# First stage of a two-block network: input products of high and low parts, own keys ahead of the context's

## The reference, cut to what matters

```python
proj = hm @ w_in                                   # 1024 x 1792: q 512, k and v 256, u 512, gate 512
q = rms_norm(proj[..., :512].reshape(b, n, 8, 64), q_g)
k, v = split_kv(proj[..., 512:768], k_g)
q, k = apply_rope(q, ...), apply_rope(k, ...)
k, v = concatenate([context's k, v], [k, v])       # context_kv(hcn, w_in, k_g): the same 256 columns
attn = block_attention(q, k, v)
g = u * sigmoid(gate)
g = silu(layer_norm(depthwise_conv(g, conv_w) + conv_b, ln_g, ln_b))     # 31 taps
out = concatenate([attn, g], -1) @ w_out
```

## Time and profile before

| | us |
|---|---|
| median of 3 runs (lowest, highest) | 1674.82 (1673.35, 1675.28) |
| the profiled execution | 1671.44 |
| its span in the trace | 1669.6 |
| PE, DVE, ACT, POOL busy in the span | 1471.2, 481.2, 339.5, 110.6 |
| first product of the changed part starts | 36.76 |
| first scores of the loop start | 105.62 |
| first use of an expert chunk | 233.29 |

### The profile page before, as it was taken

How to read it: one execution, slowest core, us unless ns; L and a number is a source line. 1 busy time by engine, 2 the same in 40 slices (tenths; PEclk the granted TensorE clock), 3 DMA queues, 4 the chain that set the end, 5 groups by cost and what they waited for, 6 DMA issues and landing times. The chain is left out here.

```text
span 1669.6 us, 17591 instructions
## 1 busy us (share of the span) xinstructions
PE 1471.2 (88%) x7708; PEld 824.5 (49%) x7708; DVE 481.2 (29%) x732; ACT 339.5 (20%) x515; POOL 110.6 (7%) x109
## 2 busy tenths in 40 slices
PE   4999979889888899789798878978888999999999
PEld 2755642232232343289532323323324767788897
DVE  1496540100100000156500001001004754345443
ACT  1122410000000000143200000000003645544442
POOL 0000000000000000010000000000003044330000
PEclk9999989999989999999799999999999999999999
DMA  9989959999999999996399999999999844244510
GB/s 374 410 359 413 410 216 429 414 429 427 416 428 427 412 428 429 407 398 234 126 418 422 427 430 419 429 427 423 428 424 355 291 175 149 104 148 168 189 51 26
DMA packets 93298, 563.06 MB, mean 337 GB/s; under 512 B 8048, under 2 KB 9448, under 8 KB 53670
## 3 DMA queue, kind: packets, MB, share of 16 engines
q1 hardware_dynamic: 89504, 551.77, 81.2%
q0 software_dynamic: 2384, 9.42, 1.6%
q10 hardware_dynamic: 1334, 0.75, 0.2%
HBM read 558.74 MB, written 3.17 MB: 337 GB/s over the span
## 5 line engine op out<-in xcount | busy, mean ns | idle before, releaser
L2207 PE MATMUL ps<-ring,scratch 128*32 128x512 f32 x2048 | 434.6, 610 | 54.4 <-DMA ring<-in_moe_w_up 26.1
L2207 PEld LDWEIGHTS ps<-ring,scratch 128*32 128x32 f32 x2048 | 129.2, 112 | 346.7 <-issue 339.5
L2186 PE MATMUL ps<-ring,scratch 128*32 128x512 f32 x1024 | 205.8, 603 | 29.7 <-DMA ring<-in_moe_w_down 29.7
L1927 PE MATMUL ps<-ring_parts,scratch_parts 128*128 128x512 f32 x656 | 186.6, 402 | 5.0 <-DVE xT_parts L1189 1.4
L1927 PE MATMUL ps<-scratch_parts,ring_parts 128*128 128x256 f32 x704 | 146.0, 282 | 0.0
L1927 PEld LDWEIGHTS ps<-ring_parts,scratch_parts 128*128 128x128 f32 x656 | 122.4, 189 | 33.1 <-DVE xT_parts L1189 1.6
L2186 PEld LDWEIGHTS ps<-ring,scratch 128*32 128x32 f32 x1024 | 50.3, 111 | 160.8 <-issue 107.8
L607 ACT ACTIVATE ring_parts<-ring 128x2048 fp32r<-128x2048 f32 x56 | 106.4, 1919 | 93.1 <-PE ps L1927 86.6
L460 DVE TENSOR_TENSOR ring_parts<-ring,ring_parts 128x2048 fp32r<-128x2048 f32 x46 | 105.6, 2296 | 54.9 <-ACT ring_parts L607 53.8
L1927 PEld LDWEIGHTS ps<-scratch_parts,ring_parts 128*128 128x128 f32 x704 | 114.7, 189 | 0.3
L1519 DVE TENSOR_TENSOR scratch<-ps,gate_bc 128x512 f32<-128x512 f32 x16 | 11.1, 692 | 250.9 <-PE ps L2186 250.9
(11 more groups left out here) (393 smaller groups left out, 1552.1 us busy)
## 6 DMA issues: line engine op xcount, KB each, us to landing
ring<-in_moe_w_gate SPq DMA_DIRECT2D x64, 2048.0 KB, 30.0
ring<-in_moe_w_up SPq DMA_DIRECT2D x64, 2048.0 KB, 17.9
ring<-in_moe_w_down SPq DMA_DIRECT2D x64, 2048.0 KB, 30.1
ring<-in_ada_w SPq DMA_DIRECT2D x24, 2048.0 KB, 15.3
ring<-in_mlp_w SPq DMA_DIRECT2D x16, 2048.0 KB, 8.7
ring<-in_sc_w_in SPq DMA_DIRECT2D x6, 2048.0 KB, 21.5
ring<-in_w_in SPq DMA_DIRECT2D x6, 2048.0 KB, 20.7
ring<-in_xattn_wkv SPq DMA_DIRECT2D x4, 2048.0 KB, 35.5
```

The source lines that it names most:

```text
L1927: last = mm(out, lhs[x], rhs[y], start=start and n == 0, stop=stop and n == 2)
L2186: last = mm(ps[32 * j:32 * j + 32, banks[half], :], src[:, k, CAP * j:CAP * (j + 1)], w[:, e, col:col + 512], start=(k == 0), stop=(k == K ...
L2207: last = mm(ps[32 * j:32 * j + 32, banks[half], :], src[:, k, CAP * j:CAP * (j + 1)], w[e][:, 0, col:col + 512], start=(k == 0), stop=(k = ...
```

## The change

The six products of this stage become products of high and low parts. Each 512-column chunk is taken in two halves (`IN_HALVES`, numbered 0 to 6): u, gate (first 256 columns each), u, gate (second), q (first and second 512 rows), k and v. For each half ACT makes the high part (`in_high(n)`, 128 x 2048, after half n - 2 is used, since there are two buffers), and DVE (n = 1, 2) or POOL (n = 0, 3, 4, 5, 6) the low part in place (`in_low(n)`), then PE multiplies. xT is split too, by ACT (`pairs_high`) and DVE for x, by ACT and POOL for the context. The taps run by channel halves: the first gated half, 40 taps, the second gated half, the context's norm, 26 taps, then 12 more behind the rope. The order of the chunks is `ada0b` ahead of `ev_kv`. The own keys are multiplied first, then PE runs `ada(1, c)`, then the context's keys. The layer norm's sums go to steps 6 and 10 and to banks 7 and 6.

```diff
-STREAM = [("ada0a", 4), ("ev_u", 1), ("ev_gate", 1), ("ev_q", 1), ("ev_kv", 1), ("ada0b", 4),
+STREAM = [("ada0a", 4), ("ev_u", 1), ("ev_gate", 1), ("ev_q", 1), ("ada0b", 4), ("ev_kv", 1),
...
-        TAPS_Q, TAPS_KV, TAPS_LOOP = 35, 12, 8
+        TAPS_FIRST, TAPS_Q, TAPS_KV, TAPS_LOOP = 40, 26, 12, 8
+        MEAN_AT, CENTER_AT, SQUARE_AT, VAR_AT, ROOT_AT, SCALE_AT = 6, 8, 9, 10, 12, 14
...
+        def in_low(eng, ops, n):
+            w, lo, hi = in_half(n)
+            eng.wait_ge(sem("in_high"), n + 1)
+            if n:
+                eng.wait_ge(sem("in_low"), n)
+            ops.tensor_tensor(lo, w, hi.bitcast(F32), ALU.subtract).then_inc(sem("in_low"), 1)
...
ACT
+            def in_high(n):
+                w, lo, hi = in_half(n)
+                arrived(act, FIRST[IN_HALVES[n][0]])
+                if n > 1:
+                    in_done(act, n - 2)
+                elif n == 0:
+                    act.wait_ge(sem("norm_T"), 4)
+                nc.scalar.activation(hi, w, ACT.Copy).then_inc(sem("in_high"), 1)
             squares("x", h, xT_rows)
+            in_high(0)
             transposed("x", xT)
+            pairs_high("x", xT, in_hi)
+            in_high(1)
...
+            in_high(2)
...
+            gates(0)
+            in_high(3)
+            in_high(4)
+            gates(1)
+            in_high(5)
+            in_high(6)
...
                 if not w:
+                    transposed("ctx", cT)
+                    pairs_high("ctx", cT, xT_r)
                     act.wait_ge(sem("inverses"), 1)
POOL
             rms("x")
+            in_low(pool, nc.gpsimd, 0)
             rms("ctx")
+            for n in range(3, len(IN_HALVES)):
+                in_low(pool, nc.gpsimd, n)
+            for b in range(4):
+                c = slice(2 * b, 2 * b + 2)
+                pool.wait_ge(sem("x_high"), 4 * SPLIT_INPUTS.index("ctx") + b + 1)
+                nc.gpsimd.tensor_tensor(in_hi[:, c, :], cT[:, c, :], xT_r[:, c, :].bitcast(F32), ALU.subtract)\
+                    .then_inc(sem("x_split"), 1)
DVE
             transposed("x", xT)
-            normed("ctx", ctx_rows, ctx_rows)
+            for b in range(4):
+                c = slice(2 * b, 2 * b + 2)
+                dve.wait_ge(sem("x_high"), b + 1)
+                nc.vector.tensor_tensor(xT_r[:, c, :], xT[:, c, :], in_hi[:, c, :].bitcast(F32), ALU.subtract)\
+                    .then_inc(sem("x_split"), 1)
+            in_low(dve, nc.vector, 1)
+            in_low(dve, nc.vector, 2)
...
-            taps_left = [(k, c) for k in range(CONVK) for c in range(CT)]
+            taps_left = [(k, 2 * j + c) for j in range(2) for k in range(CONVK) for c in range(2)]
...
+            gated(0)
...
+            taps(TAPS_FIRST)
+            gated(1)
+            normed("ctx", ctx_rows, ctx_rows)
             dve.wait_ge(sem("gpad"), 2)
             taps(TAPS_Q)
+            in_done(dve, 6)
             transposed("ctx", cT)
-            taps(TAPS_KV)
...
+            taps(TAPS_KV)
             head_norms(10, 10, 12, sq_ctx, 20)
PE
+            half_used(in_columns(0, 4))
+            half_used(in_columns(1, 6))
...
+            used(in_columns(2, 5))
+            used(in_columns(3, 7))
+            pe.wait_ge(sem("norm_ss"), 4)
+            half_used(in_rows(4))
+            used(in_rows(5))
 
             pe.wait_ge(sem("gpad"), 2)
             pe.wait_ge(sem("cv_gate"), 2)
             transposes("ctx", ctx_rows)
-            arrived(pe, FIRST["ev_kv"])
-            pe.wait_ge(sem("cw"), 1)
-            kv_rows(2, xT).then_inc(sem("own_kv"), 1)
-            normed_columns("ctx")
-            used(kv_rows(3, cT))
-
-            pe.wait_ge(sem("ev_rows"), 10)
+            pe.wait_ge(sem("in_low"), 7)
+            pe.wait_ge(sem("param_cols"), 2)
+            half_used(kv_rows(2, (in_hi, xT_r)))
             for c in range(4):
                 ada(1, c, 3)
+            pe.wait_ge(sem("ev_rows"), 2)
+            input_split("ctx")
+            used(kv_rows(0, (xT_r, in_hi)))
+
+            pe.wait_ge(sem("ev_rows"), 10)
```

More of the change, by code:

```diff
@@ L434, in halves, with in_half, in_done @@
                 yield n, w, lo, hi
+        def in_half(n):
+            name, half = IN_HALVES[n]
+            slot, hi = slot_of(FIRST[name]), evw_hi[n % 2]
+            if name == "ev_q":
+                s = slice(SLOT // 2 * half, SLOT // 2 * (half + 1))
+                return ring[:, slot, s], ring_r[slot][:, s], hi
+            w, lo = (v.rearrange("p (k n) -> p k n", k=KD)[:, :, 256 * half:256 * half + 256] for v in (ring[:, slot, :], ring_r[slot]))
+            return w, lo, hi.rearrange("p (k n) -> p k n", k=KD)
+        def in_done(eng, n):
+            if n in IN_USED:
+                eng.wait_ge(sem("half_used"), IN_USED[n])
+            else:
+                whole(eng, IN_HALVES[n][0])
+        def in_low(eng, ops, n):
[4 more added lines that the diff above has]
+            ops.tensor_tensor(lo, w, hi.bitcast(F32), ALU.subtract).then_inc(sem("in_low"), 1)
         def ev_half(j, p):
@@ L514, in _ @@
             sp.dma_start(ctx_rows, a["ctx"][0].rearrange("(t p) d -> p t d", p=P)).then_inc(sem("ctx_in"), 16)
+            modulations(1)
             columns("ev_kv", evw, 1, width=256, col0=512)
-            for g in range(1, len(ADA)):
+            for g in range(2, len(ADA)):
                 modulations(g)
@@ L640, in _, with gates @@
             act.dma_start(glam[:, :], a["cst_i"]).then_inc(sem("first_params_in"), 16)
-            whole(act, "ev_gate")
-            for j in range(2):
+            def gates(j):
+                in_done(act, (1, 3)[j])
                 nc.scalar.activation(flat(sg[:, 2 * j:2 * j + 2, :]), pb(6 + j), ACT.Sigmoid).then_inc(sem("cv_gate"), 1)
-            whole(act, "ev_q")
+            act.wait_ge(sem("ctx_in"), 16)
+            for t in range(NT):
+                if t:
+                    act.wait_ge(sem("norm_ss"), 2 * NORMS.index("ctx") + t)
+                nc.scalar.activation(ctx_junk, ctx_rows[:, t, :], ACT.Square,
+                                     accum_out=ss[:, NORMS.index("ctx"), t:t + 1]).then_inc(sem("norm_ss"), 1)
+            gates(0)
[4 more added lines that the diff above has]
+            in_high(6)
+            in_done(act, 5)
             for t in range(NT):
@@ L1276, in _, with gated @@
             link(nc.vector.memset(gpad[:, :, edge + N:PADW], 0.0))
-            whole(dve, "ev_u")
-            for j in range(2):
+            def gated(j):
+                in_done(dve, (0, 2)[j])
                 dve.wait_ge(sem("cv_gate"), j + 1)
@@ L1914, in to_rows @@
                 return last
-            def to_columns(i, rhs, banks):
-                for c in range(4):
-                    for k in range(KD):
-                        last = mm(ps[:, banks[c // 2], N * (c % 2):N * (c % 2 + 1)], slot8(i)[:, k, P * c:P * (c + 1)],
-                                  rhs[:, k, :], start=(k == 0), stop=(k == KD - 1))
-                return last
             def split_product(out, lhs, rhs, start, stop):
@@ new lines, in in_rows @@
+            def in_rows(n):
+                w, lo, hi = in_half(n)
+                pe.wait_ge(sem("in_low"), n + 1)
+                half = IN_HALVES[n][1]
+                for t in range(NT):
+                    s = slice(P * t, P * (t + 1))
+                    for kk in range(4):
+                        k, c = 4 * half + kk, slice(512 * kk, 512 * kk + 512)
+                        last = split_product(pb(t), (in_hi[:, k, s], xT_r[:, k, s]), (hi[:, c], lo[:, c]), k == 0, k == KD - 1)
+                return last
@@ L2003, in kv_rows @@
+            def kv_rows(bank, x):
+                w, lo, hi = in_half(6)
+                for t in range(NT):
+                    s = slice(P * t, P * (t + 1))
                     for k in range(KD):
-                        last = mm(ps[:, bank, 256 * t:256 * t + 256], lhs[:, k, P * t:P * (t + 1)], slot8(i)[:, k, 0:256],
-                                  start=(k == 0), stop=(k == KD - 1))
-                return last
-            i = FIRST["ev_u"]
-            arrived(pe, i)
-            used(to_columns(i, xT, (4, 5)))
+                        last = split_product(ps[:, bank, 256 * t:256 * t + 256], (x[0][:, k, s], x[1][:, k, s]),
+                                             (hi[:, k, :], lo[:, k, :]), k == 0, k == KD - 1)
+                return last
@@ L2093, in _ @@
                 ev_transposed(n)
+                if n == NQ + 1:
+                    pe.wait_ge(sem("cv_centered"), 1)
                 if n:
```

100 lines of the change are left out of this document (55 added, 45 removed).

## The result

| | us |
|---|---|
| kernel after, median of 4 runs (lowest, highest) | 1709.35 (1703.61, 1709.86) |
| kernel before, beside it, median of 4 (lowest, highest) | 1674.09 (1672.29, 1675.28) |
| ratio, 95% interval | 1.0202 (1.019 to 1.0215) |
| profiled execution, its span | 1709.86, 1708.1 |

Slower by 35.3 us. The forecast was 1697.2 with 1678 to 1709; the number of the prediction's third way was 1708. The median lies at the upper edge of the range, and 12 us above the forecast.

The account below looks back on a forecast made before the run. The weight stream bounds nearly all, but the first expert chunk's use moves the end; late start, standing taps and later chain outweigh PE's saving: first scores 128.0 for 105.6, +22.4 us on 1674.8 gives 1697.2, range 1678 to 1709.

Parts of the forecast that it names:

- third way: Rival, first taps: the whole row of 40 holds POOL, low 3 starts at 71.9; +33.5 us, 1708; chance 0.1.
- likeliest case: Taps before the scores: they stand while POOL makes each low part; +22.4 us, own range 1692 to 1703; chance 0.49.
- What moves the end: First use of an expert chunk, 233.3 us: whatever moves it moves the end by as much; some 10 us slack.
- PE's saving: PE's products before the scores: 45.4 us in place of 56.3, 11 saved if nothing makes PE wait.
- The start: Start of the products: x's low parts wait for POOL until 40.6, PE starts at 41.3, 4.5 us late.
- A PE that waits for landing weights would be something I have not foreseen.: Closing sign, on PE's waits: waiting for landing weights would be unforeseen; no size given.
- moving `ada0b` ahead of `ev_kv`: Chunk order before the loop: moving the four chunks ahead costs nothing, the stream having slack until the expert chunks.
- I take it that each gets in behind the tap that is running: POOL's four 4.58 us subtractions among DVE's 40 taps: each enters after the running tap and the taps then stand.
- the layer norm's places cost nothing: the loop's waits do not stand there: Layer norm's new steps in the loop of 16 heads: claimed to cost nothing.
- a rigid block: Loop of 16 heads and what follows: taken as unchanged in length, PE's work there left alone.
- From own keys to scores: Head norms to rope 12.4 us plus 2 for POOL and ACT, taps 4.8, then 4.8 less 0.9; scores at 128.0.

Follow-up runs that it names:

- x4c: x4b with no taps between the own keys' rope and the context's keys, 8 taps per loop step, layer norm back in steps 10 to 12: 1674.33 us.
- x4b: Kernel after with low parts 3 to 6 on DVE, convolution weights awaited alone, taps redistributed (nine per loop step), convolution's mean in step 7: 1682.9 us.
- m1: Separate kernel, no network: one POOL subtraction released by tap 5 of DVE tap rows; POOL 4.5 to 4.7 us, row of 40 from 15.9 to 20.2.
- x2: Kernel after, but PE's wait before transposing the convolution's weights is for their four transfers, not all seven: 1698.7 us.
- m2: Separate kernel: POOL released by tap 3 to 42 of 60-tap DVE rows; 4.7 to 4.8 us at tap 3, all 15 later ones stood to the row's end.
- x8: Kernel after with every fourth of the 66 taps waiting for the one just ahead: 1703.9 us.
- x9: Kernel after with the layer norm's steps back at 10 to 12 of the loop and both sums in bank 6: 1702.7 us.
- m3: Separate kernel: POOL released by taps 4 to 7, or by tap 20 of varied DVE rows; change between tap 5 and tap 6.

## Why the prediction was right, and where it was not

Slower was forecast, and slower it is. The size was not right: 35.3 us for 22.4. It is above the likeliest case's own range (1692 to 1703) and at the edge of the wide one, which reaches to 1709 only for the sake of a rival with a chance of 0.1.

**What moves the end** held: the span follows the first expert chunk (+40.2 and +38.5 in the kernel after, +2.8 and +0.9 in x4c).

**PE's saving** held: in x4b, halves 2 to 5 ran without a stop from 54.50 to 77.20, 5.7 us each, as the term had it.

**The start** came at 39.56 where 41.3 was said. The mechanism held: the first low part of x stood from 37.02 until POOL was through. `ev_u` was there by 32.4, not 34.1, which is most of the difference. The Trainium skill, "SBUF — State Buffer", § Who interferes with whom, has it that the second one to issue waits until the first is through. m1's taps and x2's agree, four standings of 4.35 us in x2. For low 4 the rule would give one tap's wait; it was 15 taps, 73.47 to 79.46, and there the measurement decides.

**The step that failed first** is one that is not in the sum: "A PE that waits for landing weights would be something I have not foreseen." ACT's copies of half 0 and of x stand ahead of the seven parameter transfers on its queue. These were issued 4 us later, moved more slowly beside the stream, and landed some 9 us after PE wanted them. Of ACT's steps the prediction counted the copies and not the transfers behind them, and moving `ada0b` ahead of `ev_kv` it put at nothing, which is open. x2 puts the price at 10.7 us, with the two holds in it. Without it the forecast stands, by the mechanism named likeliest: 1698.7 for 1697.2. Here too there is luck: the scores came 1.6 us earlier than said, what follows them took more, and the span of x2's profiled execution is 29.1 above the one before.

**"I take it that each gets in behind the tap that is running"** held for rows younger than some 6 taps (m1, m2, x2) and fell for older ones: low 4 and low 6. The third way, in which the taps hold POOL for the whole row, had the right mechanism for these two, and by luck the right sum, 1708: it has low 3 held until 71.9, which really ran at 55.90 while DVE stood for the parameters. It priced the hold at 11 us above turns (33.5 - 22.4); x8 shows 3 to 6. The two norms, which the prediction has as instructions of 0.7, stood 8 us for POOL besides.

**"the layer norm's places cost nothing: the loop's waits do not stand there"** failed, by some 3 to 9 us (x9 and the rows under it). The steps 12 and 14 are where the last maxima are made, and "a rigid block" with them: the loop was 69.7 and not 66.6.

**From own keys to scores** held: head norms 111.83 to the rope's end at 126.5 is 14.7 us (12.4 + 2 said), and on to the scores 9.2 (4.8 + 4.8 - 0.9 = 8.7 said).

**What the change could have brought** is not shown. PE saves 5 us of busy time ahead of the scores in x4c, and DVE has 19 more. x4c still starts its products 3 us later than the kernel before (39.81 for 36.76), since the low parts of x wait there for POOL's low 0; with the other losses found here taken away it is level with the kernel before. None of the versions tried beats it. The 4.8 us from the rope's end to the scores in the kernel before are no bound on what could be won, as DVE's head norms themselves start only when PE has made the own keys.

Open: the parts do not add up singly (17.1, 10.7, 4.3 and 3.2, or 8.9 and 6.1 by the spans, overlap), and whether the lower clock from 130 to 150 costs anything with DVE unloaded was not tried. Nor was the old order of `ada0b` and `ev_kv`, nor a version in which only u and gate are multiplied in parts: the low part of x takes x's place, so q and the keys have no whole x left.

## What to carry to other kernels

Count the transfers that stand behind an instruction put ahead of them on a queue, small ones too, and look at what the stream has beside them: issued at 41, they landed at 62. A step that POOL takes from a DVE that is busy with taps or norms in SBUF costs DVE its whole length: 4.35 us of standing against 2.29 to do it itself. And an operation whose result is wanted late has a place that costs: put it where DVE has no maximum due, not in the last steps.

## What was not expected of the hardware

A row of scalar_tensor_tensor on DVE, 128x256 with both tensors in SBUF and no gap, lets a subtraction of POOL in only while it is young: released by tap 5 or earlier POOL got in at the next tap and DVE stood (6 of 6 plain rows in m1 to m3), by tap 6 or later it waited for the row's end (17 of 17, up to 20.9 us). A wait for the last tap, or a memset, after every 6 taps makes it young again; using four channels in turn does not. DVE is not slowed by the one that it keeps out.

The clock of a PE that is busy without a gap can still fall: 0.66 over 10 us with PE busy 10.09 of 10.10, some 16 us after a wait of 1.42 us at which it had fallen once. Where that wait was 0.22 it stayed at 1.00 (3 of 3 executions), where it was 1.42 it fell this second time in 5 of 8; what decides between the 5 and the 3 is open. The 10 us then held 45 matmuls in place of 58, 3 us lost.
